# Layer 0's attention-gate part of the modulation, summed by VectorE from four early loads

## The reference, cut to what matters

```python
c_act = jax.nn.silu(c)
for l in range(DEPTH):
    mod = (c_act @ ada_w[l] + ada_b[l])[:, None, :]
    sh1, sc1, gt1, sh2, sc2, gt2 = jnp.split(mod, N_MOD, axis=-1)
    h = rms_norm(x, norm1_g[l]) * (1.0 + sc1) + sh1
    x = x + gt1 * token_mixer(h, ...)
    h = rms_norm(x, norm2_g[l]) * (1.0 + sc2) + sh2
    x = x + gt2 * conv_gated_mlp(h, ...)
return rms_norm(x, final_g)
```

## Time and profile before

| | |
|---|---|
| median of 3 runs | 980.9 us (980.74 to 980.96) |
| the profiled execution | 982.01 us, its span 980.2 us |
| TensorE busy | 959.2 us, 98% of the span |
| VectorE busy | 776.9 us, 79% |
| ScalarE busy | 517.7 us, 53% |
| mean granted clock of TensorE | 0.994 |
| moved by DMA | 202.04 MB, 206 GB/s mean |

### The profile page before, as it was taken

The page is one execution under the profiler, slowest core; times in us unless marked ns, Lnnn a source line. Parts: engine busy times, 40 slices in busy tenths (PEclk is TensorE's granted clock), DMA queues, the critical chain, the costliest instruction groups (busy, mean ns, idle before and its releaser), DMA issues.

```text
span 980.2 us, 18743 instructions
## 1 busy us (share of the span) xinstructions
PE 959.2 (98%) x7747; PEld 911.4 (93%) x7747; DVE 776.9 (79%) x1154; ACT 517.7 (53%) x726; POOL 18.1 (2%) x23
## 2 busy tenths in 40 slices
PE   6899999999999999999999999999999999999997
PEld 4789899999998999999989999999999899999997
DVE  2549889987986888889885798999799578888634
ACT  3384365558435666654255544565744555665432
POOL 5000000000000000000000000000000000000001
PEclk9899999999999999999999999999999999999999
DMA  9966355666783556957994434446769355555551
GB/s 313 324 224 223 127 162 191 212 219 213 259 299 130 174 191 196 342 173 280 393 346 130 151 124 140 124 132 216 255 227 332 130 172 173 175 192 181 184 172 44
DMA packets 140979, 202.04 MB, mean 206 GB/s; under 512 B 3416, under 2 KB 114148, under 8 KB 140900
## 3 DMA queue, kind: packets, MB, share of 16 engines
q1 hardware_dynamic: 140564, 200.68, 60.5%
q10 hardware_dynamic: 336, 0.21, 0.1%
HBM read 199.83 MB, written 1.05 MB: 205 GB/s over the span
## 4 chain that ended last, share of the span: by engine, by line
PE 93%; DVE 4%; DMA 1%; ACT 1%; issue 0%; SPq 0%; DVEq 0%
PE PB L1525 20%; PE PB L1527 19%; PE PB L1526 19%; PE PB L1548 2%; PE PB L1549 2%; PE PB L1550 2%; PE SC L1525 2%; PE SC L1527 2%; PE SC L1526 2%; PE ST L1504 1%; DMA ada_pre<-in_ada_w 1%; PE ST L1585 1%; PE OB L1527 1%; PE TR L1527 1%; PE SC L1681 1%; PE TR L1525 1%
## 5 line engine op out<-in xcount | busy, mean ns | idle before, releaser
L1525 PE MATMUL PB<-hH,wH 128*128 128x256 f32 x1360 | 389.9, 287 | 1.0 <-DVE wL L988 1.0
L1527 PE MATMUL PB<-hH,wL 128*128 128x256 f32 x1360 | 384.7, 283 | 0.0
L1526 PE MATMUL PB<-hL,wH 128*128 128x256 f32 x1360 | 384.7, 283 | 0.0
L988 DVE TENSOR_TENSOR wL<-raw,wH 128x2048 fp32r<-128x2048 f32 (+3 forms) x152 | 323.0, 2127 | 74.8 <-ACT wH L700 70.4
L700 ACT ACTIVATE wH<-raw 128x2048 fp32r<-128x2048 f32 (+3 forms) x152 | 268.4, 1782 | 100.0 <-DMA raw<-in_w_down 53.3
L1525 PEld LDWEIGHTS PB<-hH,wH 128*128 128x128 f32 x1360 | 260.6, 192 | 6.5 <-issue 4.9
L1526 PEld LDWEIGHTS PB<-hL,wH 128*128 128x128 f32 x1360 | 260.7, 192 | 0.8 <-issue 0.7
L1527 PEld LDWEIGHTS PB<-hH,wL 128*128 128x128 f32 x1360 | 260.6, 192 | 0.0
L1097 DVE SCALAR_TENSOR_TENSOR buf<-G,vec,buf 128x256 f32<-128x256 f32 x240 | 98.2, 478 | 0.3
L1318 DVE SCALAR_TENSOR_TENSOR ups<-PB,vec,ups 128x254 f32<-128x254 f32 (+1 forms) x176 | 72.6, 475 | 18.0 <-ACT ups L859 18.0
L867 ACT ACTIVATE gH<-ups 128x512 f32 (+1 forms) x22 | 13.9, 632 | 86.7 <-DVE ups L1325 86.7
(11 more groups left out here) (289 smaller groups left out, 1704.0 us busy)
## 6 DMA issues: line engine op xcount, KB each, us to landing
raw<-in_w_in SPq DMA_DIRECT2D x48, 1024.0 KB, 5.4
raw<-in_w_up SPq DMA_DIRECT2D x44, 1024.0 KB, 5.1
ada<-in_ada_w SPq DMA_DIRECT2D x38, 1024.0 KB, 8.2
raw<-in_w_down SPq DMA_DIRECT2D x22, 1024.0 KB, 4.9
ada_pre<-in_ada_w SPq DMA_DIRECT2D x8, 1024.0 KB, 13.5
raw<-in_w_o SPq DMA_DIRECT2D x8, 1024.0 KB, 5.7
raw<-in_w_out_diff SPq DMA_DIRECT2D x4, 1024.0 KB, 5.2
raw<-in_w_out_conv SPq DMA_DIRECT2D x4, 1024.0 KB, 5.4
```

The lines of the kernel that those rows point to most:

```text
L988: dve.tensor_tensor(wL[s][:, 0:size], raw[s][:, 0:size], wH[s][:, 0:size].bitcast(F32), ALU.subtract).then_inc(w_lo[s], 1)
L1525: pe.matmul(out, a, xh(k), start=first and k == 0, stop=False, skip_group_check=True)
L1526: pe.matmul(out, a, xl(k), start=False, stop=False, skip_group_check=True)
L1527: ins = pe.matmul(out, b, xh(k), start=False, stop=last and k == kt - 1, skip_group_check=True)
```

## The change

The four products of layer 0's q = 0 leave TensorE. `ADA_STEPS` and `ADA_LOADS` lose their first four entries. Four loads of the same 4 MB go to four places (`early_ws`: `ada[0]`, two new buffers that lie where oB and oA lie later, and `ada_u`), issued behind the weight loads of chunks 2, 3, 4 and 5. The second waits for all four groups' products, because its place and the two after it overlap `ada_pre`. VectorE makes eight passes: two at step 2, two at step 3, four at step 4, each ahead of that step's low part. At chunk 12 TensorE collects the sum from `early_ws[3]` with eight matmuls against ones (`reduce_early`); ScalarE's eviction falls away in layer 0. The load of the fifth ada block (chunk 15) waits for the first two passes, since they read `ada[0]`; the late part's first load (chunk 28) waits for the collecting, since it overwrites `ada_u`. The counts of `ada_used`, `ada_out` and `ada_in` are shifted to match.

```diff
--- before.py
+++ after.py
@@ -104,13 +104,17 @@
 ADA_PART = 4
 ADA_PARTS = [2, 3, 4, 5]
 ADA_ONCE, ADA_GAP, ADA_CHUNKS = 8, 12, 16
-ADA_STEPS = [1, 4, 7, 10, 14, 18, 22, 25] + [None] * 8
-ADA_LOADS = [n + 1 for n in ADA_STEPS[:ADA_ONCE]] + [None] * 4 + [39, 40, 42, 41]
+ADA_STEPS = [None] * 4 + [14, 18, 22, 25] + [None] * 8
+ADA_LOADS = [None] * 4 + [n + 1 for n in ADA_STEPS[4:ADA_ONCE]] + [None] * 4 + [39, 40, 42, 41]
 ADA_BUF = [0] * ADA_GAP + [1, 2, 3, 0] * 2
 ADA_EVICT_AT = {12: 0, 29: 1, UP + 4 * UP_LOOPS: 3}
 ADA_REDUCE_AT = {12: 0, 29: 1, 39: 2, UP + 4 * UP_LOOPS + 1: 3}
 assert len(ADA_STEPS) == ADA_CHUNKS and UP + 4 * UP_LOOPS == 59
 
+EARLY_Q = 0
+EARLY_LOADS, EARLY_STEPS = [2, 3, 4, 5], [2, 2, 3, 3, 4, 4, 4, 4]
 
 
 LATE_Q = 2
@@ -130,12 +134,12 @@
     late = 4 * (a >= ADA_CHUNKS)
     if ADA_BUF[a]:
         return l * 5 + 1 + late
-    return a + 1 if a < ADA_ONCE else l * 5 + 9 + late
+    return a - 3 if a < ADA_ONCE else l * 5 + 5 + late
 
 
 def sum_loads(b):
 
-    return (1 if SUM_BUF[b] else 9) + b // 4 + 1
+    return (1 if SUM_BUF[b] else 5) + b // 4 + 1
 
 
 def ada_order(l, q):
@@ -145,12 +149,12 @@
 
 def ada_evicts(l, q):
 
-    return {0: l * 3 + 1, 1: 2, 3: l * 2 + 3}[q]
+    return {0: 3, 1: 1, 3: l * 2 + 2}[q]
 
 
 def ada_done(l, q):
 
-    return {0: l * 12 + 4, 1: 8, 3: l * 8 + 12}[q]
+    return {0: 12, 1: 4, 3: l * 8 + 8}[q]
 
 
 V_N1, V_N2, V_ADAB, V_QG, V_KVG, V_CB, V_LNG, V_LNB, V_SUB, V_FB = 0, 8, 16, 64, 67, 69, 73, 77, 81, 82
@@ -319,6 +323,9 @@
 
         mix = ExitStack()
         G = sb("G", [P, 24, T], F32, mix)
+        early_o = ExitStack()
+        ada_oB, ada_oA = (sb(n, [P, 2, 1024], F32, early_o) for n in ("ada_oB", "ada_oA"))
+        early_o.close()
         oBH = sb("oBH", [P, HEADS_D, T], F32R, mix)
         oBL = sb("oBL", [P, HEADS_D, T], F32R, mix)
         oAH = sb("oAH", [P, HEADS_M // 2, T], F32R, mix)
@@ -347,6 +354,7 @@
         late_ada.close()
         mix.close()
         late_ws = [ada_u, ada[0], ada[1], ada[2]]
+        early_ws = [ada[0], ada_oB, ada_oA, ada_u]
         late_sum = latq[:, 0:CT, :].rearrange("p k t -> p (k t)")
 
 
@@ -403,6 +411,7 @@
         ada_in = [sem(f"ada_in{i}") for i in range(4)]
         ada_used, ada_out = sem("ada_used"), sem("ada_rows_out")
         ada_sum = sem("ada_summed")
+        early_in, early_added = [sem(f"early_in{i}") for i in range(4)], sem("early_added")
         late_in, late_added = [sem(f"late_in{i}") for i in range(4)], sem("late_added")
         ada_pre_in = [sem(f"ada_pre_in{i}") for i in range(2 * GROUPS)]
         pre_used, pre_out, pre_full, pre_read = (
@@ -508,8 +517,10 @@
             def load_ada(l, a):
 
                 part, i = ADA_PARTS[a // ADA_PART % len(ADA_PARTS)], a % ADA_PART
-                if 0 < a < ADA_ONCE:
-                    sp.wait_ge(ada_used, a)
+                if a == ADA_PART:
+                    sp.wait_ge(early_added, 2)
+                elif a < ADA_ONCE:
+                    sp.wait_ge(ada_used, a - ADA_PART)
                 elif ADA_GAP <= a < ADA_CHUNKS:
                     sp.wait_ge(late_added, 8 * (l + 1))
                 elif a:
@@ -541,7 +552,7 @@
 
                 part, i = SUM_PARTS[b // ADA_PART], b % ADA_PART
                 if b < ADA_PART:
-                    sp.wait_ge(ada_used, ADA_ONCE + b + 1)
+                    sp.wait_ge(ada_used, ADA_PART + b + 1)
                 else:
                     sp.wait_ge(ada_sum, 2 * (b - 3))
                 at = SUM_BUF[b]
@@ -552,13 +563,25 @@
             def load_late(l, i):
 
                 part = ADA_PARTS[LATE_Q]
+                if i == 0 and l == 0:
+                    sp.wait_ge(mi_full, 1)
                 if i == 1 and l == 0:
-                    sp.wait_ge(ada_used, ADA_ONCE)
+                    sp.wait_ge(ada_used, ADA_PART)
                 sp.dma_start(late_ws[i][:, :, :],
                              ada_v[:, l * DT + 2 * i:l * DT + 2 * i + 2, 1024 * part:1024 * (part + 1)]).then_inc(late_in[i], 16)
 
+            def load_early(i):
+
+                part = ADA_PARTS[EARLY_Q]
+                if i == 1:
+                    sp.wait_ge(pre_used, GROUPS)
+                sp.dma_start(early_ws[i][:, :, :],
+                             ada_v[:, 2 * i:2 * i + 2, 1024 * part:1024 * (part + 1)]).then_inc(early_in[i], 16)
+
             def ada_behind(l, n):
 
+                if l == 0 and n in EARLY_LOADS:
+                    load_early(EARLY_LOADS.index(n))
                 if n in LATE_LOADS:
                     load_late(l, LATE_LOADS.index(n))
                 a = ADA_LOADS.index(n) if n in ADA_LOADS else None
@@ -665,7 +688,10 @@
                 q = ADA_EVICT_AT.get(n)
                 if q is None:
                     return
-                if q == 1:
+                if q == EARLY_Q:
+                    if l > 0:
+                        ada_evict(ada_done(l, q))
+                elif q == 1:
                     if l < LAYERS - 1:
                         ada_evict(ada_done(l, q))
                 else:
@@ -1116,6 +1142,8 @@
                                              ALU.subtract).then_inc(m_lo, 1)
 
             def mixer_step(l, n):
+                if l == 0:
+                    early_steps(n)
                 if n == MLA + 1:
                     weights(l, SCORES_AT[n - 1])
                 if n < OUTS:
@@ -1240,6 +1268,21 @@
                     if n == WO - 2:
                         merged_low(l, n)
 
+            def early_steps(n):
+
+                for j in range(8):
+                    if EARLY_STEPS[j] != n:
+                        continue
+                    i, row = divmod(j, 2)
+                    w, c, to = early_ws[i][:, row, :], c_col[:, j, 0:1], early_ws[i][:, 0, :]
+                    dve.wait_ge(early_in[i], 16)
+                    if j == 0:
+                        ins = dve.tensor_scalar(to, w, c, None, ALU.mult)
+                    else:
+                        dve.wait_ge(early_added, j)
+                        ins = dve.scalar_tensor_tensor(to, w, c, early_ws[(j - 1) // 2][:, 0, :], ALU.mult, ALU.add)
+                    ins.then_inc(early_added, 1)
+
             def late_steps(l, n):
 
                 for j in range(8):
@@ -1268,7 +1311,7 @@
                         if l < LAYERS - 1:
                             ada_end(ADA_PARTS[q], ada_order(l, q), vec)
                     elif at + 1 == n:
-                        ada_end(ADA_PARTS[q], ada_order(l, q), vec, 2 if q == LATE_Q else 1)
+                        ada_end(ADA_PARTS[q], ada_order(l, q), vec, 2 if q == LATE_Q or (l, q) == (0, EARLY_Q) else 1)
                         if q == 2:
                             dve.wait_ge(mi_read, ada_order(l, q))
                             link(dve.scalar_tensor_tensor(gs[:, 1, :], mod[:, 4 * DT:5 * DT], 1.0, vec[:, V_N2:V_N2 + DT],
@@ -1480,6 +1523,14 @@
                                     stop=True, skip_group_check=True)
                 ins.then_inc(mi_full, 1)
 
+            def reduce_early():
+
+                after(early_added, 8)
+                for m in range(DT):
+                    ins = pe.matmul(MI[:, 2 * m:2 * m + 2], early_ws[3][:, 0, m * P:(m + 1) * P], ones[:, 0:2], start=True,
+                                    stop=True, skip_group_check=True)
+                ins.then_inc(mi_full, 1)
+
             def reduce_late(l):
 
                 after(mi_read, l * 6 + LATE_Q)
@@ -1701,6 +1752,8 @@
                         reduce_ada(ada_evicts(l, q))
                 elif q == LATE_Q:
                     reduce_late(l)
+                elif (l, q) == (0, EARLY_Q):
+                    reduce_early()
                 elif q is not None:
                     reduce_ada(ada_evicts(l, q))
                 if n in SUM_REDUCE_AT:
```

## The result

The changed kernel is slower. In the first comparison it took 985.06 us (median of 6, 982.63 to 985.73) against 981.0: ratio 1.0037, interval 1.0027 to 1.0048. It was compared twice more: 983.97 us (11 runs, ratio 1.0026, 1.0017 to 1.0036) and 983.27 us (8 runs, 1.0021, 1.0011 to 1.0031). Over all 25 runs the median is 983.97 us, with 982.6 to 986.2 as the ends; the kernel before, in 27 runs beside the last experiments, has 981.18 with 980.7 to 982.6. So the loss is 2 to 4 us, and the changed kernel spreads twice as wide as the old one.

What follows compares the result with a forecast made beforehand. TensorE was taken to bound the kernel, so lateness counts in full: scores +2.6, steps removed behind them -2.0, collecting +0.9, low clock +2.9 make +4.4 us on 980.9, forecast 985.3 us, range 979.2 to 986.5.

Steps and rivals of the forecast that it cites:

- the clock's term: Behind the first scores: the hole lowers TensorE's clock to half for 6.8 us, which loses 2.9 us.
- Removed from TensorE, and collecting: Layer 0's attention-gate part on TensorE: four steps go, -4.0 us; the new collecting adds 0.9 us; -3.1 us at most.
- Passes on VectorE, costless: Eight passes, 11 us at most, lie in VectorE's idle time, ending 1.4 us before the cover ends, at no cost.
- Chunk 5's weights 3.4 us late (2.5 to 3.8): DMA queue: two more MB ahead need 5.4 us, 1.6 us fit a hole, so these weights land later.
- The chain to the scores: From chunk 5's landing at 57.4 over ScalarE and VectorE to TensorE's first scores: 0.8 us of slack.
- TensorE waits 4.6 us for the scores: TensorE is ready at 83.4, rotations end at 88.0; the scores start 2.6 us later than before.
- rival A: At the first scores: late scores and a low clock behind them, 984.4 to 985.7, up to 986.3; chance 0.52.
- rival B: At the first scores: late scores but the clock held, +0.6 to +1.9 us, 981.5 to 982.8; chance 0.25.

Runs made afterwards that it cites:

- short execution: The changed kernel without further edit, the profiled execution of the first comparison, the shortest of its six: 982.63 us, span 980.8.
- long execution: The changed kernel without further edit, run a third time and profiled in a longer execution: 984.66 us, span 982.9.
- the small passes: The changed kernel with VectorE's eight passes cut to 8 words a partition, all their waits kept: 983.86 us.
- the spread version: The changed kernel with the second to fourth early loads behind the weights of chunks 5, 6 and 7, passes at steps 2, 4 and 11: 978.33 us, ratio 0.9973.
- evicting first: The changed kernel with ScalarE evicting chunk 2's latents before the high part of chunk 4, not behind it: 984.83 us.
- Filling: The changed kernel with 12 idle matmuls ahead of chunk 3 and 12 ahead of the first scores: 982.8 us, ratio 1.0016.
- the tables first: The changed kernel with ScalarE's small evictions and tables of angles ahead of chunk 5's high part, six passes ahead of its low part: 981.23 us, ratio 0.9998.
- the spread version with the later normalizing: The spread version with layer 0's latents normalized on VectorE behind the second rotation, not ahead of chunk 7's low part: 981.48 us.

## Why the prediction was right

985.3 us was forecast, slower with 0.62; 985.06 us was measured first, and 984.0 over all runs. Both lie inside the range and the sign is the forecast's, but the clock's term had another size and one wait was not foreseen. That the first median came within 0.3 us of the forecast is in part luck: the forecast was +4.4 us, the sum of the terms as measured is +1.1 us in the short execution and +2.9 in the long one, and the difference of the medians over all runs is 2.8.

- *Removed from TensorE, and collecting*: as worked out. The collecting takes 1.68 us. With the scores 2.2 us late the sum of the short execution is 2.2 - 2.0 + 0.9 = +1.1; its span is 0.6 us longer than the old one's. The profile before is not a short one itself (982.01 us against a median of 980.9, with the low stretch of 6.8 us in its start), so a short execution stands closer to it than the medians stand to each other. For the long execution the sum is 2.7 - 2.0 + 0.9 + 1.3 of clock = +2.9, and its span is 2.7 us longer.
- *Passes on VectorE, costless*: right, with 1.3 us of cover left where 1.4 was worked out; shown by the small passes.
- *Chunk 5's weights 3.4 us late (2.5 to 3.8)*: 3.0 in the profile of the short execution, 3.5 in the long one. Measured from the issue it is 4.3 us (12.6 against 8.3), since this execution had issued them 1.3 us earlier. The long one issued them 1.9 us after the short one and had them 0.5 us after it. So a good start of TensorE hardly moves this landing while the queue is full, and in the spread version's profile it did move it.
- *The chain to the scores*: right in place and length (27.2 us + 0.8 of slack; eight profiles and the second one of the changed kernel agree to 0.1 us). Scores at 88.0 were forecast, 87.6 to 88.1 were measured.
- *"TensorE waits 4.6 us for the scores"*: wrong as put. I followed chunk 4's weights only to TensorE's chunk 4 and not to what ScalarE does behind their high part. The eviction of chunk 2's latents stands there, and holds up chunk 3 by 1.2 to 2.0 us. The wait at the scores itself was 1.5 and 3.1 us. The sum was not touched, since the chain to the scores is the longer one; evicting first moved the wait and gained nothing.
- *The clock, 2.9 us behind the scores*: mis-sized. In the profiles of the changed kernel the low stretch is 3.4 us and not 6.8, 1.3 to 1.5 us; it stands behind the scores, where it costs, only in the long execution; in the short ones it stands behind chunk 3, where it is covered by the wait that follows. Filling gives 1.2 us in the median. So the long execution is rival A with half its stretch, and the short ones have rival B's price for another reason than B gave: the clock did fall, at a place where it cost nothing. I had put the two as alternatives for the kernel. The rule of the Trainium skill cited in the prediction ("TensorE: Matmul & The Clock Gate", "HAM oscillation — how this bites in real kernels") would give 3.4 x 0.5 = 1.7 us for such a stretch; the windows of the long execution give 1.3, and the two durations of a matmul 3.4 x (1 - 0.12/0.21) = 1.5, so the trace stays somewhat under the rule.

How far 4 us in the first comparison and 2 to 3 in the later ones come from the mix of long and short executions stays open: three executions of the same kernel were compared, not their distribution. The profiles put the parting in the start, ahead of 46 us; what sets the length of the low stretch there stays open.

## What to carry to other kernels

A transfer issued early "because the queue has room" is in front of everything issued after it: count the bytes ahead of the next transfer that somebody waits for, and follow what that engine does behind its wait, in order, to the first point where the bounding engine needs it. Taking work from the bounding engine is worth, ahead of that point, only the slack of that chain, and the whole behind it; here the same edit lost 3 us with two loads ahead of the critical weights and won 2.7 us with them behind. Where a wait is unavoidable, shorter ones ahead of a point that is late anyway were cheaper here than one long one at that point (981.2 against 982.8 us with the tables first; 984.0 against 984.8 in the changed kernel, where the intervals overlap). The profiles put the difference down to where the low clock falls.

## What the runs showed of the hardware that was not expected

The low stretch of the clock in the start had three lengths in the thirteen profiles, some 3.4, 6.8 and, in the spread version with the later normalizing, 10.2 us (21.8 to 32.1). In the kernel before it was 6.8 us, from 26.6 on, behind a wait of 2.1 us; in the changed kernel's short execution it was 3.4 us, from 28.1 on, behind one of 1.5 us for the same eviction. In the changed kernel's long execution it was 6.8 us again, behind a wait of 2.1 us. With it the start of everything after moves by over 1 us from execution to execution. A wait of 2.0 us in front of chunk 3 went with a low clock in three profiles (both short executions, and the tables first), while waits of 1.2 us (the long execution) and 1.7 us (the small passes) there did not. With twelve matmuls that nobody needs, 1.7 us in front of chunk 3 and 1.6 us at the scores, the profile has full clock from 44 to 100 us, and the times of ten of eleven executions agree to 0.6 us.
